# Banded attention: normed and split exponentials, values as the stationary tile, three heads at a time

## The reference, cut to what matters

```python
s = jnp.einsum('bnqhgd,bnkhd->bnhgqk', qb, kb) * (HEAD_DIM ** -0.5)   # 6 heads, 2 key heads, windows of 128
s = jnp.where(mask, s + bias, -jnp.inf)                               # a query tile sees its own and the previous key tile
lse = jnp.logaddexp(logsumexp(s, axis=-1, keepdims=True), sink)       # one learned sink score per head
p = jnp.exp(s - lse)
o = jnp.einsum('bnhgqk,bnkhd->bnqhgd', p, vb)                         # 64 values a head
```

## Time and profile before

| | us |
|---|---|
| median of 3 runs | 2729.76 (2728.09 to 2732.17) |
| profiled execution | 2732.24 |
| its span, first to last instruction | 2730.5 |
| TensorE busy | 2689.0 (98%) |
| VectorE busy | 1520.5 (56%) |
| ScalarE busy | 1140.6 (42%) |
| GpSimd busy | 208.7 (8%) |

### The profile page before, as it was taken

One profiled execution on the slowest core, in us unless ns is written; L12 is line 12 of the kernel. 1 busy time (PEld: TensorE's weight loads), 2 busy tenths in 40 slices (PEclk: granted clock), 3 DMA queues, 4 the chain that ended last, 5 costly groups with the idle time before them and its releaser, 6 DMA issues.

```text
span 2730.5 us, 34821 instructions
## 1 busy us (share of the span) xinstructions
PE 2689.0 (98%) x13513; PEld 2230.8 (82%) x13513; DVE 1520.5 (56%) x2670; ACT 1140.6 (42%) x2063; POOL 208.7 (8%) x323
## 2 busy tenths in 40 slices
PE   8999999999999999999999999999999999999999
PEld 7788888887888888878777888888878778888887
DVE  7756344467564444676766653343677676653343
ACT  4644222246442222465655343242465655342232
POOL 5200000002000000021122000000020121000000
PEclk9999999999999999999999999999999999999999
DMA  5113333231133333332311333333423212333332
GB/s 140 41 44 100 99 94 100 93 88 50 36 101 100 94 99 98 93 100 70 110 46 39 101 93 99 95 100 91 115 65 106 78 40 62 101 93 99 95 100 86
DMA packets 191000, 235.62 MB, mean 86 GB/s; under 512 B 12418, under 2 KB 144996, under 8 KB 190836
## 3 DMA queue, kind: packets, MB, share of 16 engines
q1 hardware_dynamic: 187572, 225.95, 27.4%
q0 software_dynamic: 2256, 5.52, 1.1%
q10 hardware_dynamic: 1008, 1.92, 0.2%
HBM read 227.05 MB, written 2.11 MB: 84 GB/s over the span
## 4 chain that ended last, share of the span: by engine, by line
PE 90%; DVE 6%; ACT 2%; issue 1%; DMA 0%; POOL 0%; ACTq 0%; DVEq 0%; POOLq 0%
PE bank L668 26%; PE bank L670 26%; PE bank L669 26%; PE bank L959 2%; PE bank L904 1%; PE bank L980 1%; DVE Wl L2288 1%; PE bank L1224 1%; PE bank L1022 1%; PE bank L981 1%; PE bank L1033 1%; PE bank L1023 1%; PE bank L889 1%; DVE STT L2644 1%; PE bank L1424 1%
## 5 line engine op out<-in xcount | busy, mean ns | idle before, releaser
L2288 DVE TENSOR_TENSOR Wl<-RAW,Wh 128x1024 fp32r<-128x1024 f32 (+4 forms) x434 | 512.0, 1202 | 322.0 <-ACT Wh L1522 321.0
L1522 ACT ACTIVATE Wh<-RAW 128x1024 fp32r<-128x1024 f32 (+4 forms) x434 | 438.4, 1033 | 398.5 <-PE bank L670 392.7
L668 PE MATMUL bank<-Hh,Wh 128*128 128x512 f32 x1104 | 448.3, 406 | 2.3 <-DVE Hl L2358 1.5
L670 PE MATMUL bank<-Hh,Wl 128*128 128x512 f32 x1104 | 431.7, 391 | 0.0
L669 PE MATMUL bank<-Hl,Wh 128*128 128x512 f32 x1104 | 431.1, 390 | 0.0
L668 PE MATMUL bank<-HA,Wh 128*128 128x512 f32 x704 | 274.2, 390 | 0.0
L670 PE MATMUL bank<-HA,Wl 128*128 128x512 f32 x704 | 273.9, 389 | 0.0
L669 PE MATMUL bank<-HA,Wh 128*128 128x512 f32 x704 | 273.9, 389 | 0.0
L670 PEld LDWEIGHTS bank<-Hh,Wl 128*128 128x128 f32 x1104 | 207.2, 188 | 44.9
L668 PEld LDWEIGHTS bank<-Hh,Wh 128*128 128x128 f32 x1104 | 208.3, 189 | 40.5 <-issue 4.8
L669 PE MATMUL bank<-A,Wh 128*128 128x512 f32 x608 | 236.5, 389 | 0.0
(11 more groups left out here) (412 smaller groups left out, 4760.2 us busy)
## 6 DMA issues: line engine op xcount, KB each, us to landing
RAW<-in_w_up_dram SPq DMA_DIRECT2D x108, 512.0 KB, 3.7
RAW<-in_w_down_dram SPq DMA_DIRECT2D x108, 512.0 KB, 3.7
RAW<-in_w_in_dram SPq DMA_DIRECT2D x86, 512.0 KB, 3.7
RAW<-in_w_gate_dram SPq DMA_DIRECT2D x44, 512.0 KB, 3.7
RAW<-in_w_out_dram SPq DMA_DIRECT2D x28, 512.0 KB, 3.7
RAW<-in_cmp_w_dram SPq DMA_DIRECT2D x16, 512.0 KB, 4.0
RAW<-in_w_o_fox_dram SPq DMA_DIRECT2D x8, 512.0 KB, 4.5
RAW<-in_w_o_nsa_dram SPq DMA_DIRECT2D x8, 512.0 KB, 3.4
```

The source lines that it names most:

```text
L668: pe.matmul(o, sh, mh, start=first, stop=False)
L670: return pe.matmul(o, sl, mh, start=False, stop=last)
L1522: sc.activation(M.Wh[:, v % NHL, 0:n], M.RAW[:, v % NRAW, 0:n], ACT.Copy).then_inc(G.w_hi, 1)
L2288: ve.tensor_tensor(M.Wl[:, v % NRAW, 0:n], M.RAW[:, v % NRAW, 0:n], M.Wh[:, v % NHL, 0:n].bitcast(F32), ALU.subtract).then_inc(G.w_lo, 1)
```

## The change

The banded attention leaves `attend` and goes through `mixing`, in 8 bundles of three heads of one tile (`swa_bundles`).

- The exponential sum of an item and its sink are added and inverted per item on VectorE (`invert`), with one exponential of the sink per item on ScalarE; GpSimd multiplies the item's exponentials by the reciprocal (`normalise`).
- The transposed exponentials are split in an upper part (ScalarE) and a lower part (VectorE), both fp32r.
- The values are split once a layer into `VS`, [upper | lower], 128 columns, and are the stationary tile; the exponentials of three heads move together, 384 columns, in two fp32r matmuls for each key block.
- The result comes out with the features on the rows, so `turn_out` and its three transposes a tile are gone. Each trio is copied by ScalarE in two instructions into `OSW` (`swa_take`), added to by VectorE in two (`swa_sum`), and after both trios of a tile split into `Hh` and `Hl` (`swa_out`).
- The branches for the banded attention go out of `attend`, and `out0` waits for the new semaphore `swa_lo`.

```diff
+def swa_bundles(l):
+    trios = [[(t, g, 3 * g + x) for x in range(3)] for pair in PAIRS for g in range(2) for t in pair]
+    return Bundles(f"swa{l}", trios, lambda t, g, h: f"{t}{g}", lambda t, g, h: h % 3 * P)
...
+def trio(g, o):
+
+    even, odd = (slice(0, 3, 2), slice(1, 2)) if g == 0 else (slice(1, 2), slice(0, 3, 2))
+    b = o[:, 0:3 * P].rearrange("p (x c) -> p x c", c=P)
+    return ((0, even, slice(0, 2) if g == 0 else slice(2, 3)), (64, odd, slice(0, 1) if g == 0 else slice(1, 3))), b
...
# TensorE
-            yield from attend(f"swa{l}", softmax_items(6), 6, swa_scores, lambda g, h, k: M.V1[:, k, 64 * (h // 3):64 * (h // 3) + 64],
-                              first_mix=swa_values)
+            yield from mixing(swa_bundles(l), swa_scores, lambda t, g, h, k: M.VS[:, k, g, :], swa_values)
...
             if k == 0:
-                for t in range(NT):
-                    pe.wait_ge(*K.drained(f"swa{l} x{t}0"))
+                pe.wait_ge(G.swa_lo, NT * l + NT)
...
# ScalarE, mixing
+            if banded:
+                nm = M.STT[:, 0, t, h:h + 1]
+                sc.activation(e, e, ACT.Exp, bias=nm, accum_out=M.STT[:, 1, t, h:h + 1]).then_inc(*ex.up())
+                sc.activation(M.STT[:, 3, t, h:h + 1], M.SNK[:, 6 * int(tag[3]) + h:6 * int(tag[3]) + h + 1], ACT.Exp, bias=nm).then_inc(G.sink_ex, 1)
+                return
...
-            yield from attend(f"swa{l}", softmax_items(6), 6, (M.Hh, 0))
+            sc.wait_ge(*K.points[f"mla{l}", 23])
+            sc.wait_ge(*K.drained(f"vt{l}"))
+            sc.activation(M.VS[:, :, :, 0:64], M.V1[:, :, :].rearrange("p s (g d) -> p s g d", d=64), ACT.Copy).then_inc(*hi.up())
+            yield from mixing(swa_bundles(l), take=swa_take, finish=swa_out)
+
+        def swa_take(t, g, h):
+            o = f"swa{l} o{t}{g}"
+            sc.wait_ge(*K.full(o))
+            halves, b = trio(g, M.bank[K.of(o)])
+            for r0, x, j in halves:
+                i = sc.activation(M.OSW[r0:r0 + 64, j, t * P:(t + 1) * P], b[0:64, x, :], ACT.Copy)
+            i.then_inc(G.whole, 1)
+
+        def swa_out(t, g, h):
+            if g:
+                for x in range(2):
+                    sc.wait_ge(*K.drained(f"swa{l} o{t}{x}"))
+                sc.activation(M.Hh[:, 0:3, t * P:(t + 1) * P], M.OSW[:, :, t * P:(t + 1) * P], ACT.Copy).then_inc(*hi.up())
...
# VectorE, mixing
+            if banded:
+                if B.freed_by(i) is not None:
+                    ve.wait_ge(*K.full(f"{tag} t{B.freed_by(i)}"))
+                e, top, sk = B.exps(M, i), M.STT[:, 2, t, h:h + 1], 6 * int(tag[3]) + h
+                ve.tensor_tensor_reduce(e, M.bank[K.of(name)][:, 0:e.shape[1]], M.BIAS[:, h, (0 if t else P):256], 1.0, M.SNK[:, sk:sk + 1],
+                                        ALU.add, ALU.max, top).then_inc(*K.empties(name))
+                ve.wait_ge(*K.drained(name))
+                ve.tensor_scalar(M.STT[:, 0, t, h:h + 1], top, -1.0, None, ALU.mult).then_inc(*mx.up())
+                return
...
         def invert(i):
             t, g, h = items[i]
-            ve.wait_ge(*K.drained(f"{tag} s{i}"))
+            if banded:
+                total = M.STT[:, 1, t, h:h + 1]
+                ve.wait_ge(*ex.due())
+                ve.wait_ge(*sink_ex.due())
+                ve.tensor_tensor(total, total, M.STT[:, 3, t, h:h + 1], ALU.add).then_inc(*own.up())
+                ve.wait_ge(*own.now())
+            else:
+                ve.wait_ge(*K.drained(f"{tag} s{i}"))
...
-            yield from attend(f"swa{l}", softmax_items(6), 6, (M.Hh, M.Hl, 0))
+            ve.wait_ge(*K.full(f"mla{l} t23"))
+            ve.wait_ge(*K.points[f"mla{l}", 23])
+            lower(M.VS[:, :, :, 64:128], M.V1[:, :, :].rearrange("p s (g d) -> p s g d", d=64), M.VS[:, :, :, 0:64]).then_inc(G.v_lo, 1)
+            yield from mixing(swa_bundles(l), add_up=swa_sum, finish=swa_out)
+
+        def swa_sum(t, g, h):
+            o = f"swa{l} o{t}{g}"
+            ve.wait_ge(*whole.due())
+            halves, b = trio(g, M.bank[K.of(o)])
+            for r0, x, j in halves:
+                y = M.OSW[r0:r0 + 64, j, t * P:(t + 1) * P]
+                i = ve.tensor_tensor(y, y, b[64:128, x, :], ALU.add)
+            i.then_inc(*K.empties(o))
+
+        def swa_out(t, g, h):
+            if g:
+                q = slice(t * P, (t + 1) * P)
+                lower(M.Hl[:, 0:3, q], M.OSW[:, :, q], M.Hh[:, 0:3, q]).then_inc(G.swa_lo, 1)
...
# GpSimd
         window_rows(l)
+        normalise(swa_bundles(l), lambda t, g, h: M.ONE[:, 0:1])
```

More of the change, by code:

```diff
@@ L883, in turn @@
             b = fresh(f"{tag} t{i}")
[L884 to L887 removed]
+            pe.wait_ge(*K.drained(f"{tag} s{i}"))
             for k in range(nb):
@@ L1686, in turn @@
             name = f"{tag} t{i}"
-            if kind == "swa" and h == H - 1:
-                x = M.STT[:, 3, t, 0:H]
-                sc.wait_ge(*sink.due())
-                sc.activation(x, x, ACT.Exp).then_inc(G.sink_ex, 1)
-            if kind == "swa" or i % 2 == 0:
+            if i % 2 == 0:
                 sc.wait_ge(*K.full(name))
@@ L1731, in mixing @@
         tag, items = B.tag, B.items
+        banded = tag[:3] == "swa"
         def head(i):
@@ L1787, in packed_k @@
         i.then_inc(*hi.up())
-    sink = Count(G.sink)
     sc.dma_start(M.CST[:, 0:P], a["cst"][:, 0:P]).then_inc(G.ident_in, 16)
@@ L2540, in head @@
             name = f"{tag} s{i}"
[L2541 to L2542 removed]
+            b, nm = M.bank[K.of(name)], M.STT[:, 0, t, h:h + 1]
             ve.wait_ge(*K.full(name))
[L2544 to L2552 removed]
+            ve.tensor_reduce(nm, b[:, 0:w], AX.X, ALU.max, negate=True).then_inc(*mx.up())
         def turn(i):
@@ L2557, in turn @@
             name = f"{tag} t{i}"
-            if kind == "swa" and h == H - 1:
-                ve.wait_ge(G.mx, mx.n)
-                ve.tensor_tensor(M.STT[:, 3, t, 0:H], M.SNK[:, 6 * l:6 * l + 6], M.STT[:, 0, t, 0:H], ALU.add).then_inc(G.sink, 1)
-            if kind != "swa" and i % 2:
+            if i % 2:
                 ve.wait_ge(*K.full(name))
@@ L2571, in mix @@
                 sums = M.STT[:, 1, t, 0:H]
-                if kind == "swa":
-                    ve.wait_ge(*sink_ex.due())
-                    ve.tensor_tensor(sums, sums, M.STT[:, 3, t, 0:H], ALU.add).then_inc(*own.up())
-                    ve.wait_ge(*own.now())
-                else:
-                    ve.wait_ge(*K.drained(f"{tag} s{i + 2}"))
+                ve.wait_ge(*K.drained(f"{tag} s{i + 2}"))
                 ve.reciprocal(fac, sums).then_inc(*own.up())
```

34 lines of the change are left out of this document (9 added, 25 removed).

## The result

The changed kernel takes 2750.9 us (median of 4 runs, 2749.2 to 2751.7) against 2728.9 of the kernel before beside it: the ratio is 1.0076, interval 1.0064 to 1.0089. It is slower, as forecast, but by 22 us and not by 8, and outside the range of 2724 to 2745. The profiled execution lasted 2749.2 us.

A forecast was written before the change was run, and what follows sets the result against it. VectorE, with waits behind ScalarE, was to bound the banded stage: 35.5 us work, 5.7 and 1.0 waits make 42.2, then 8.3 to `out0`; +4.1 a layer, +8.2 in two, from the 2729.8 median gives 2738 us, range 2724 to 2745.

The forecast's parts named there:

- The start: Ahead of the banded stage's first maximum: splitting the values first costs 0.7 us with nothing to hide it.
- the end: From the banded stage's last maximum to `out0`: 8.3 us, against 11.0 in the kernel before.
- Rival C: Banded stage: VectorE keeps up, TensorE stays the bound; -6 to -7.5 us a layer, 2715 to 2718; chance 0.1.
- Sum 42.2 us: VectorE from first to last maximum: 35.5 us of work, 5.7 waiting behind ScalarE, 1.0 for weight copies.
- 8 x 0.7: VectorE's waits for ScalarE's copies at six trios and two output splits, 0.7 us each, given as 5.7 us.
- two signs of being wrong: VectorE's 35.5 us mis-sized by more than a tenth, or ScalarE later than the forecast has it.
- should go too: TensorE's 1.4 us of bank waits in the stage vanish, an output bank being opened and closed in one tick.
- TensorE's saving: TensorE's work in the banded stage, removed matmuls and transposes against added 384-column matmuls: -6.2 us a layer.
- dear first matmul of a group: First 512-column `outa` matmul after fp32 ones drops from 0.32 to 0.23 us: 2.4 us a layer saved.
- B: Banded stage: VectorE bounds but its waits behind ScalarE vanish; -2.6 us a layer, 2724.5; chance 0.2.
- D: Banded stage: GpSimd's multiplication enters the loop; at 1.18 us each, 4.3 us a layer more, 2747; chance 0.2.
- The rule weighed: VectorE with two SBUF inputs contends with GpSimd reading SBUF: up to 0.6 us per weight split, 5 us in two layers.

The follow-up runs named there:

- e5: Changed kernel with ScalarE copying a trio of values ahead of the exponential of the same tick, not behind it: 2743.7 us, ratio 1.0051.
- e6: Changed kernel with the transposes' bank handed back behind that of the scores of the same tick: 2747.8 us, ratio 1.0067.
- e17: e15 with e11's sum and inversion on GpSimd and e13's extra tick between scores and transposes: 2733.3 us, ratio 1.0009.
- e1: Changed kernel with VectorE's trio additions one tick later, the output's split moving along on all three engines: 2747.5 us, ratio 1.0064.
- e7: Changed kernel with both edits, e5's trio copy and e6's order of banks: 2739.9 us, ratio 1.0037.
- e10: e7 with VectorE splitting an output (Hl) in the next tick, behind its maximum and reciprocal: 2740.4 us, ratio 1.0029.
- e8: Changed kernel with GpSimd multiplying only the first column of each banded item: 2749.9 us, ratio 1.0072.
- e13: e7 with the transposes of a banded item and all that follows one tick later: 2739.0 us, ratio 1.0032.
- e2: Changed kernel without adding the sink's exponential to the sum of each banded item on VectorE: 2747.4 us, ratio 1.0065.
- e9: e7 without adding the sink's exponential to the sums on VectorE: 2737.2 us, ratio 1.0026.
- e11: e7 with GpSimd instead of VectorE adding the sink's exponential and inverting each banded item's sum: 2739.6 us, ratio 1.0035.
- e12: e10 and e11 together, output split a tick later and sum and reciprocal on GpSimd: 2738.4 us, ratio 1.0028.
- e14: e13 with e11's sum and reciprocal of the banded items on GpSimd: 2737.9 us, ratio 1.0026.
- e16: e15 with e11's sum and reciprocal of the banded items on GpSimd: 2737.0 us, ratio 1.0027.
- e15: e7 with ScalarE making the upper part of an output (Hh) ahead of the exponential of its tick: 2737.7 us, ratio 1.0030.

## Why the prediction was wrong

**Right.** TensorE stopped being the bound of the stage, and the direction with it. The start (first maximum 0.76 us later against the first group of `outa`; 0.72 forecast), the end (8.75; 8.3), the wide tick without extras (1.20; 1.21), the 384-column matmuls (0.175 at full clock), the first matmul behind them (0.24; 0.23), the 512-column addition (0.60; 0.61), the output split (0.475; 0.48) and GpSimd's 0.554 and 0.449 came as worked out. Rival C is out.

**The step that failed** is the sum of VectorE's stretch, "Sum 42.2 us": it measured 47.75, 5.5 more a layer, and with 0.5 at the end that is the error: 12 us in two layers, where 2750.9 is 12.9 above 2738. (8 x 0.7 is 5.6 and not 5.7, which changes nothing.) Two terms of it were too small. Work was 38.4 and not 35.5: a trio's two additions cost 0.76 and not 0.54 (six of them in the stretch, 1.3 us), the sum and reciprocal 0.29 and not 0.27, a wide lower half 0.38 and not 0.34, a wide head 0.62 and not 0.60, together 1.5 more with small change. Of the two additions the next instruction starts 0.44 us behind the one with 256 columns and 0.31 behind that with 128; I had 0.34 and 0.20, from the durations of splits less 0.08, and nothing is taken off here. Waits were 9.3 and not 6.7: 5.3 for 6 trio copies, up to 1.1 each where I had 0.7; 1.5 for `Hh` in 2 outputs; and 2.5 for `PTh`, the weight copies, a late bank and the sink, where I had 1.0. Of the two signs of being wrong that the forecast names, the first didn't come (38.4 is 8% above 35.5, under a tenth), the second did: ScalarE was later.

**What was missing in the argument.** I counted one list and its waits, and took the waits as given by ScalarE alone. e5 shows that place, the copy behind the exponential, to be the largest single cause found (3.4 us a layer). But the same loop went on through TensorE and the queue of banks (e6, 1.1; both together 5.3), and I had written that bank waits "should go too" when an output's bank is closed in its tick. It was opened in a bank that VectorE's list reaches late. Nor did I give TensorE's idle time any effect on its clock. It fell inside the second of two waits of up to 2 us, to a mean of 0.92 between the marks, and that ate TensorE's saving in the ledger (55.0 of work, 51.5 in e17 at full clock). In e1 the same idle time left it full in one layer, so what brings it down stays open.

**Luck in e7.** With both orders mended, the stretch (42.55 us) and the time (2739.9) are nearly the forecast's 42.2 and 2738. That does not confirm its sum: it is 38.5 of work and 4.0 of waits, where the forecast had 35.5 and 6.7, so two errors cancel.

**TensorE's saving** was mis-sized too, though it didn't decide: 3.3 us a layer at full clock in e17 (54.8 to 51.5; 2.4 to 4.0 in the other layers at full clock, e1 and e10), not 6.2. The terms, before and in e17: the fp32 values were worth 7.7 us, as I had it; their successors cost 5.4 (4.9 forecast). The dear first matmul of a group became cheaper by 1.7 a layer (0.307 to 0.265 in the mean of 40), not 2.4, and some of its price went elsewhere: the third matmul, ahead of the transposes, starts 0.28 before its successor where it was 0.24, 1.5 us in 40.

**Rivals.** B, its waits gone, 2724.5: e7 took nearly all the waits for the copies away (0.6 us left) and measured 2739.9, so B fails as a number: VectorE's 38.4 us of work stayed (38.5 in e7), and TensorE still waited 7.7 for the product. D's price of 1.18 us did not occur in the changed kernel (the row was of 384 columns, where 0.66 is usual, and the banded products have 256 or 128), but its loop did. TensorE waited 7.7 us between the marks for the product at ordinary prices, though by the paths of e8 and e13 this alone was worth 0.6 to 1.4 us a layer.

**Busy shares.** I expected VectorE busy over 85% of the stretch; it was 36.5 of 47.75 us (76%). TensorE was busy as much in it (36.8 us, 77%). When no engine is busy much more than three quarters of a stretch, a loop through several is a rival, and it should have had a number of its own.

## What to carry to other kernels

When work moves from one engine to three that meet each tick, add up the loop and not the list: for each wait, ask which instruction of which tick releases it, what is queued ahead of that one on its engine, and go on until you are back; banks handed round in a queue are a link like any other. The cheap repairs are orders: issue what another engine waits for ahead of what nobody waits for (e5, 7 to 8 us by moving one call), and hand banks back in the order in which they are emptied (e6, 2 us by the path, 4 by the medians). Work taken off VectorE (e2, e9, e11) gave a fifth to two fifths of its length, or nothing, while such a loop stood.

## What the runs showed of the hardware

The rule weighed ahead of the result, by which one of VectorE and GpSimd is blocked while the other works on SBUF, did not act in the changed kernel: 18 wide products with a mean of 0.554 us in each layer, none long. Its weight splits began 0.04 and 0.15 us before the end of a product, or met none. In e1 the order of the list put a product beside a weight split with two SBUF inputs, and it took three times as long (timeline of GpSimd and VectorE in e1):

```profile
189.02 1.62 POOL L3497 TENSOR_SCALAR P<-P,STT,ONE 128x256 f32<-128x256 f32 x1 [1.76 <-DVE STT L2673]
...
189.16 1.22 DVE L2312 TENSOR_TENSOR Wl<-RAW,Wh 128x1024 fp32r<-128x1024 f32 x1
```

1.62 is the usual 0.55 and 1.07 more, with 1.22 us of VectorE beside it, four times in e1, at the same two places in both layers. That the two contend agrees with the Trainium skill (SBUF — State Buffer, Who interferes with whom). The row of the product begins 0.14 us ahead of the subtraction, which kept its 1.22; but a product of one column already takes 0.34 us (e8), and spans on GpSimd are rough, so which of them asked first is not settled. In e11, e12, e14, e16 and e17 the row of a 1024-column split begins 0.1 us ahead of the product's, and the product takes 1.53 to 1.56 us. Beside the 0.55 us of `Hl` it took 0.8 in e10 and 0.95 to 0.98 in e15. In these and in e1 and e13 VectorE kept its time, and the product ended some 0.3 to 0.45 us behind VectorE's instruction. The forecast's estimate of 5 us in two layers from it was for an overlap that the changed kernel's order of instructions did not have; what it cost in the reordered kernels was not measured.

On GpSimd one column costs 0.34 us in a multiplication by two scalars, 0.26 in an addition and 0.55 in a power, against 0.16 for a one-column instruction on VectorE. On ScalarE the exponential of one column with a bias takes 0.28 us.
